# A scan mixer computed in blocks of four time steps, inside a fused two-block decoder kernel

## Chip, cores and metric

One core of a Trainium2 chip. The time is device microseconds of one execution of the whole program (both decoder blocks, two layers each, 256 tokens, float32 results). Engines are named as in the profile: PE is the matrix engine, PEld its weight loads, DVE the vector engine, ACT the scalar engine, POOL GpSimd, SP the engine that issues most transfers.

## The reference, cut to what matters

The first block (`first_block`, two layers of attention with a selector, a state-space mixer and a gated MLP) isn't touched by the change. The second block has three mixers side by side on one normalised input: latent attention, gated linear attention (GLA) and S5, a diagonal state-space scan:

```python
def s5_mixer(u, lam_re, lam_im, b_re, b_im, c_re, c_im, d, log_dt, w_glu, b_glu):
    lam = lax.complex(jnp.minimum(lam_re, -1e-4), lam_im)          # 32 groups x 64 states
    lam_bar = jnp.exp(lam * jnp.exp(log_dt)[:, None])
    b_bar = ((lam_bar - 1.0) / lam)[..., None] * lax.complex(b_re, b_im)
    bu = ...                       # (L, 32 groups, 64 states), complex, from 16 channels a group
    _, states = lax.associative_scan(diag_combine, (lam_bar, bu), axis=1)  # x[t] = lam_bar x[t-1] + bu[t]
    y = Re(states) @ c_re - Im(states) @ c_im + d * u
    y = jax.nn.gelu(y)
    return y * jax.nn.sigmoid(y @ w_glu + b_glu)
```

There are 256 steps, 512 channels (32 groups of 16) and 2048 complex states (16 tiles of 128 partitions, each two groups).

## The kernel before, in words

**Stages.** `Plan` cuts all weight matrices into 658 units in eight stages, `STAGES`: a b a b (first block, layers 0 and 1), then c d c d (second block). Stage c holds the mixers, d the MLP. Stage c has 79 units. Ten of them, the `native` ones, multiply plain float32; each of the others is 24 matmuls (high times high, high times low, low times high part of a float32 product split in two). A unit's weights come by DMA into `ring` (5 slots); ACT copies them to `WH` (function `hi`, rounding them to the high part), DVE subtracts to get `WL` (function `lo`, line 1403), PE multiplies. `WH` and `WL` have four halves, so `hi` of unit u+3 waits for PE to have finished unit u-1. Where `x.pool` holds, POOL makes `WL` in DVE's place (line 2115); that is so for 11 units of each stage b.

**Order.** Each engine's program is one loop over the units. At unit u it does its part of the unit, the evacuation of groups that ended one to three units ago, and then the steps of the mixers that `agenda` lists for u. `C_TICKS` and `A_TICKS` name the units at which each mixer advances, counted from the stage's first unit. Each mixer is a generator on each engine (`s5`, `gla`, `norms`, `heads`), and a `yield` ends its step for this tick. So all engines walk the same list, and each runs its queue strictly in order. A step that waits holds up everything behind it on its engine, `hi` and `lo` of the next units too.

**S5 before.** The setup `s5set` (in the stage ahead: stage b for layer 0, stage d for layer 1; ticks 48 to 62 and 38 to 52) makes the step's decay `r`, its turn (cos, sin), the output matrix `SC5` times the input factor, and two tables of 16 powers of the turn (lines 1925 to 1942) in `TF`. POOL's `turns` multiplies these into the 256 turns of each state tile, `CT`: 12 instructions of 128x256 for each q (lines 2101 to 2105). In stage c, `s5` takes the 16 state tiles in 8 pairs q, four ticks each (ticks 6 to 55 of 79). For each tile PE multiplies the input (`inputs`: two matmuls 32x128 by 256 columns), DVE turns the result back (lines 1956 to 1959), scans it over 256 steps twice (line 1962), turns it forward (lines 1970 to 1973), and PE multiplies with `SC5` (`y`, 32 columns of output for each tile). DVE then adds the skip term (line 1981), and gelu and the gate follow (lines 1985 to 1991, ACT's `tanh`). The result is first read by `glu` at unit 65.

**Lines named later.** 1519 and 1520 sum squares for the next stage's norm; 1536 spreads `pe`, the shared rope part of the keys (unit 9), to eight heads; 1540 evacuates `b1`, GLA's output projection, and frees its bank; 1781 is a step of GLA; 1606 scales the attention weights; 955 loads an activation table.

Of the kernel before, what the change touches and what calls it, by code (L numbers as in the profile page):

```python
# [30 lines left out]
def vec_columns():  # L31
    at, n = {}, 0
    for l in range(2):
        for name, k in VECS:
# [7 lines left out]
          ("mask", 384), ("cos2", 256), ("sin2", 256), ("scan", 256), ("invf", 1), ("eps", 1)]  # L42
# [10 lines left out]
def const_array():  # L53
# [7 lines left out]
    put["id"][:] = p == f[:, :128]  # L61
    put["ones"][:] = 1
# [117 lines left out]
def stage_c(l):  # L180
# [20 lines left out]
    return (su + cq + ckv + pe + glr + gq + gk + gv + gr + uq + uk + uv + g[1] + b[1] + g[0] + g[2] + b[0] + glu  # L201
# [11 lines left out]
class Plan:  # L213


    def __init__(self):
# [31 lines left out]
        for x in self.units:  # L248
            b = self.base[x.stage + 1] - self.base[x.stage]
            x.pool = x.split and STAGES[x.stage][0] is stage_b and x.i - self.base[x.stage] < 44 and x.i % 4 == 3  # L250
# [55 lines left out]
def turn_ticks(first, n, num, den):  # L306
# [19 lines left out]
    "s5": turn_ticks(6, 32, 8, 5) + [57, 58, 59, 60, 61],  # L326
}
S5_TICKS = {stage_b: [48, 50, 52, 54, 56, 58, 60, 62], stage_d: [38, 40, 42, 44, 46, 48, 50, 52]}


def program(nc, io):
# [3 lines left out]
    with ctx:  # L335
# [78 lines left out]
        for nm, n in (("QH", 2048), ("KH", 2048), ("VV", 1024), ("OA", 1024), ("CQ", 768), ("CKV", 512), ("GQ", 512),  # L414
# [6 lines left out]
        a2["OG"], a2["MG"] = a2["GK"], a2["GV"]  # L421
# [5 lines left out]
        SU, TF, CT = ar(a2["SU"], 4, T), ar(a2["TF"], 4, 256), ar(a2["CT"], 2, 2, 512)  # L427
        SC5, SB5, SX = ar(a2["SC5"], 2, 512), ar(a2["SB5"], 2, 512), ar(a2["SX"], 512)
        SG = trig[:, 0, :].rearrange("p (a b) -> p a b", b=16)
        MG, GX, G2 = ar(a2["MG"], 8, T), ar(a2["GX"], 8, T), ar(a2["QH"], 8, T)  # L430
        BRH = [over("oah", a2["VV"], 4), over("ogh", a2["KT"], 4), over("ysh", a2["TF"], 4)]
        BRL = [over("oal", a2["OA"], 4), over("ogl", a2["OG"], 4), over("ysl", a2["CT"], 4)]
# [96 lines left out]
        def tensor_program(e):  # L529
# [154 lines left out]
            def gla(l):  # L684
                L, st = LA, 4 + 2 * l
                p.wait_ge(ev_scalar("glr", l, 0, st), wgate_in(l))
# [67 lines left out]
            def heads(l, par):  # L754
                L = (LB, LA)[par]
                m = 4 + l
                for bi in (par, par + 2):
# [8 lines left out]
            def s5(l):  # L766
                L = LC

                def inputs(q, h):
                    R = slice(32 * ((2 * q + h) % 4), 32 * ((2 * q + h) % 4) + 32)  # L770
                    p.wait_ge(ev_scalar("su", l, q // 4, 4 + 2 * l), s5_in(l))
                    for i in range(2):
# [14 lines left out]
                for q in range(8):  # L787
                    if q:
                        p.wait_ge(L.V("scan", l, q - 1, 0), L.V("scan", l, q - 1, 1))
                        y(q - 1)  # L790
# [1450 lines left out]
```

## Time and profile before

| what | value |
|---|---|
| median of 3 runs | 2397.68 us (2396.55 to 2397.8) |
| the profiled execution | 2392.69 us |
| its span, first to last instruction | 2390.6 us |
| PE busy | 2229.1 us, 93% |
| DVE busy | 1783.4 us, 75% |
| ACT busy | 1350.0 us, 56% |
| POOL busy | 277.0 us, 12% |
| mean granted PE clock | 0.971 of full |

The profiled execution is the one that all rows come from. Its time stands 2.1 us above its span (start and end of the program) and 5.0 us under the median. A busy PE is one with a matmul in flight; matmuls overlap, so the time that one costs is the distance to the start of the next, and not its own duration. The stages end, by the first activation of each boundary, near 1324 us (stage c of layer 0 starts), 1666 us (its stage d), 1858 us (stage c of layer 1) and 2202 us (its stage d).

### The profile page before, as it was taken

How to read it: one execution, taken by the hardware profiler on the slowest of the kernel's cores; microseconds unless marked ns; L12 is line 12 of the kernel's file. 1: busy time of each engine (PE TensorE's matmuls, PEld its weight loads, DVE VectorE, ACT ScalarE, POOL GpSimd, SP SyncE). 2: the span in 40 equal slices, each digit the busy share in tenths (PEclk: the TensorE clock that was granted, in tenths of full speed). 3: DMA queues.
4: the chain of work that ended last, by engine and by line, in shares of the span. 5: the costliest groups of instructions: out<-in, count | busy, mean ns of one | idle time of the engine just before them, and what ended most of it. 6: DMA issues, size and time to landing. Idle time of an engine off the chain costs nothing.

```text
span 2390.6 us, 42135 instructions
## 1 busy us (share of the span) xinstructions
PE 2229.1 (93%) x17214; PEld 2083.8 (87%) x17214; DVE 1783.4 (75%) x3196; ACT 1350.0 (56%) x2113; POOL 277.0 (12%) x308
## 2 busy tenths in 40 slices
PE   2989999999999999999999899898999999898999
PEld 2979899989998898998998875788999875788999
DVE  5898778678769877776778788876668788876653
ACT  3577886466446888854664535454554435444542
POOL 0000000022000000000211332300004232200000
PEclk9999999999999999999999998999999998999999
DMA  7555456567755554664665313244655313244554
GB/s 278 174 165 181 160 202 220 181 198 232 231 178 168 160 201 145 210 221 143 190 193 172 126 60 108 89 158 136 197 184 187 119 54 117 89 159 133 185 186 132
DMA packets 110850, 395.72 MB, mean 166 GB/s; under 512 B 12321, under 2 KB 13889, under 8 KB 110401
## 3 DMA queue, kind: packets, MB, share of 16 engines
q1 hardware_dynamic: 96768, 343.52, 44.1%
q0 software_dynamic: 12160, 44.08, 5.7%
q10 hardware_dynamic: 1728, 5.43, 0.6%
q8 instruction: 136, 2.23, 0.4%
q14 instruction: 58, 0.47, 0.1%
HBM read 391.93 MB, written 1.05 MB: 164 GB/s over the span
## 4 chain that ended last, share of the span: by engine, by line
PE 74%; DVE 14%; ACT 8%; issue 2%; DMA 1%; SPq 0%; DVEq 0%; ACTq 0%
PE bank L534 73%; ACT scr L966 3%; DVE WL L1403 3%; ACT WH L966 2%; ACT L955 2%; DMA ring<-in_w 1%; DVE arena L1467 1%; DVE scr L1656 1%; DVE arena L2022 1%; ACT arena L966 0%; DVE scr L1450 0%; DVE small L1655 0%; DVE scr L1643 0%; DVE arena L1581 0%; DVE scr L1970 0%
## 5 line engine op out<-in xcount | busy, mean ns | idle before, releaser
L966 ACT ACTIVATE WH<-ring 128x1024 fp32r<-128x1024 f32 (+1 forms) x638 | 671.1, 1053 | 865.9 <-PE bank L534 837.8
L534 PE MATMUL bank<-HTH,WH 128*128 128x256 f32 x3392 | 984.9, 290 | 39.2 <-DVE HTL L1443 12.3
L534 PE MATMUL bank<-HTL,WH 128*128 128x256 f32 x3392 | 971.2, 286 | 0.0
L534 PE MATMUL bank<-HTH,WL 128*128 128x256 f32 x3392 | 970.5, 286 | 0.0
L1403 DVE TENSOR_TENSOR WL<-ring,WH 128x1024 fp32r<-128x1024 f32 (+2 forms) x616 | 747.7, 1224 | 150.8 <-ACT WH L966 149.1
L534 PEld LDWEIGHTS bank<-HTH,WH 128*128 128x128 f32 x3392 | 662.7, 195 | 60.5 <-issue 48.9
L534 PEld LDWEIGHTS bank<-HTL,WH 128*128 128x128 f32 x3392 | 662.7, 195 | 1.7 <-issue 1.4
L534 PEld LDWEIGHTS bank<-HTH,WL 128*128 128x128 f32 x3392 | 662.3, 195 | 0.0
L955 ACT ACT_TABLE_LOAD x110 | 141.1, 1283 | 21.8 <-DMA arena<-in_crow 13.8
L534 PE MATMUL bank<-ff2h,WH 128*128 128x256 f32 x512 | 144.0, 281 | 0.0
L534 PE MATMUL bank<-ff2l,WH 128*128 128x256 f32 x512 | 143.8, 281 | 0.0
L534 PE MATMUL bank<-ff2h,WL 128*128 128x256 f32 x512 | 143.8, 281 | 0.0
L2123 POOL DMA_DIRECT2D arena<-in_wada x80 | 42.9, 536 | 840.9 <-DVE mod L2022 779.7
L534 PE MATMUL bank<-scr,cst 128*128 128x256 f32 (+2 forms) x190 | 71.8, 500 | 64.5 <-ACT scr L966 54.3
L2022 DVE CUSTOM_DVE_ANT_0 arena<-arena 128x1024 f32<-128x1024 f32 x96 | 116.4, 1221 | 9.3 <-DMA arena<-in_wada 9.3
L2101 POOL TENSOR_TENSOR arena<-arena 128x256 f32<-128x256 f32 x64 | 63.4, 990 | 505.4 <-DVE scr L1973 289.6
L1467 DVE SCALAR_TENSOR_TENSOR scr<-bank,cols,scr 128x254 f32<-128x254 f32 (+1 forms) x176 | 72.7, 476 | 49.8 <-ACT scr L966 49.8
L534 PE MATMUL bank<-arena 64*128 64x128 f32 (+8 forms) x608 | 98.5, 342 | 8.9 <-DVE arena L1981 6.7
L534 PEld LDWEIGHTS bank<-scr,cst 128*128 128x128 f32 (+1 forms) x190 | 33.6, 198 | 83.3 <-ACT scr L966 59.2
L534 PE MATMUL bank<-ff1h,WH 128*128 128x256 f32 x352 | 100.3, 285 | 0.5 <-DVE WL L1403 0.5
L534 PE MATMUL bank<-ff1l,WH 128*128 128x256 f32 x352 | 99.5, 283 | 0.0
L534 PE MATMUL bank<-ff1h,WL 128*128 128x256 f32 x352 | 99.4, 282 | 0.0
(284 smaller groups left out, 3852.1 us busy)
## 6 DMA issues: line engine op xcount, KB each, us to landing
ring<-in_w SPq DMA_DIRECT2D x620, 512.0 KB, 4.0
arena<-in_wada POOLq DMA_DIRECT2D x80, 512.0 KB, 4.6
ring<-in_w SPq DMA_DIRECT2D x16, 384.0 KB, 3.9
arena<-in_wada SPq DMA_DIRECT2D x8, 512.0 KB, 19.7
arena<-in_wada ACTq DMA_DIRECT2D x8, 512.0 KB, 22.3
ring<-in_w SPq DMA_DIRECT2D x8, 288.0 KB, 2.8
arena<-in_s POOLq DMA_DIRECT2D x4, 512.0 KB, 5.2
cst<-in_cst SPq DMA_DIRECT2D x1, 1025.0 KB, 6.5
```

Source lines behind the costliest of these rows:

```text
L534: ins = e.matmul(out, a, b, start=(start and i == 0), stop=(stop and i == len(pairs) - 1))
L955: e.add_instruction(mybir.InstLoadActFuncSet(name=f"I-{4000000 + table[1]}", act_func_set_id=need, ins=[], outs=[]))
L966: return e.activation(out, a, func, **kw)
L1403: e.tensor_tensor(half(WL, x), raw(x), half(WH, x).bitcast(F32), ALU.subtract).then_inc(lo_vector.inc(x.i), 1)
L1467: ins = e.scalar_tensor_tensor(outs[h][:, d:T], ps[:, h * T:h * T + T - d], col(name + "_w", l, (ntap - 1 - d) * nch + cs[h]), outs[h][:, ...
L1656: serial(e.match_replace(y, top, x, GONE), L.V)
L2022: e.tensor_tensor_reduce(tile, tile, silc, 1.0, 0.0, ALU.mult, ALU.add, mod[:, l, j:j + 1]).then_inc(ada_vec.inc("sum", l, j), 1)
L2101: e.tensor_tensor(o, slow(a), fast(b), ALU.mult).then_inc(S.inc(), 1)
L2123: e.dma_start(adabuf, io["wada"][before[0], before[1]]).then_inc(ada_in.inc(*before, by=16), 16)
```

## The change

S5 is computed in 64 blocks of four steps.

- The scans run over 64 block states with the decay r^4, on tiles of 8 state tiles side by side (512 columns), twice instead of sixteen times. The table of turns `TAB` has 64 entries a state, is made by DVE's `s5set` by doubling (n = 1 to 32), and POOL's `turns` is gone.
- The inputs of four steps are stacked: `U` holds 4 steps x 2 groups x 16 channels on 128 partitions and 64 columns. POOL's `powers` makes B, lam B, lam^2 B, lam^3 B (`BS`, 18 instructions of 128x256 in the stage ahead), ACT spreads them to `PADB`, PE transposes (32 transposes), ACT copies to `BT`. `CS` holds C lam^1 to C lam^4 (24 instructions of 128x256 on DVE), spread by ACT to `PADC`.
- What an output takes from inputs of its own block comes from a triangular matrix of short answers: PE makes C lam^k B (`kernel`, 32 matmuls of 32 columns), DVE masks it and adds d (`kernel_`), ACT shifts it into `TM`.
- `y` is three matmuls a tile (48 of 63 or 64 columns), ACT takes the result to `SU` (`out`, 16 copies of 32 partitions).
- Ticks: `s5` 2 to 36 instead of 6 to 61, `s5set` 4 to 56 (stage b) or 4 to 44 (stage d) in 14 steps instead of 8. `tanh` is two ACT steps of 128x512, at ticks 30 and 32, instead of four of 128x256.
- POOL clears three arena tiles of 2048 at the start of stage c, and one at unit 11; ACT's first step (tick 2) waits for the first three.
- `pe` moves from unit 9 to unit 26, between the query and the key projections.
- POOL makes `WL` for 7 units of each stage c (15, 18, 21, 33, 36, 39, 42).

```diff
-    return (su + cq + ckv + pe + glr + gq + gk + gv + gr + uq + uk + uv + g[1] + ...
+    return (su + cq + ckv + glr + gq + gk + gv + gr + uq + pe + uk + uv + g[1] + ...
+            x.pool = x.split and (STAGES[x.stage][0] is stage_b and u < 44 and x.i % 4 == 3
+                                  or STAGES[x.stage][0] is stage_c and 15 <= u < 45 and u % 3 == 0)
-    "s5": turn_ticks(6, 32, 8, 5) + [57, 58, 59, 60, 61],
+    "s5": [2, 3, 4, 5, 6, 7, 8, 9, 10, 12, 13, 14, 16, 17, 18, 19, 20, 21, 22, 24, 25, 26, 28, 30, 32, 34, 36],
-S5_TICKS = {stage_b: [48, 50, 52, 54, 56, 58, 60, 62], stage_d: [38, 40, 42, 44, 46, 48, 50, 52]}
+S5_TICKS = {stage_b: [4, 6, 8, 11, 14, 17, 20, 23, 26, 29, 33, 37, 50, 56],
+            stage_d: [4, 6, 8, 10, 12, 14, 16, 18, 20, 22, 25, 28, 38, 44]}
...
+                def inputs(h):                                   # PE, ticks 8 and 12
+                    for n in range(8):
+                        t = 8 * h + n
+                        for i in range(2):
+                            ins = mm(L.b[i][:, 64 * n:64 * n + 64], [(BT[i][:, t, :], U[:, t, :])])
+                def y(h, b):                                     # PE, ticks 18 and 24
+                        mm(b[:, 64 * n:64 * n + 64], [(TM[:, t, :], U[:, t, :])], start=(n == 0), stop=False)
+                        ins = mm(b[:, 64 * n + 1:64 * n + 64], [(PADC[0][:, t, :], xr[:, n, 0:63]),
+                                                               (PADC[1][:, t, :], xi[:, n, 0:63])], ...)
...
+                p.wait_ge(L.G("zero", l), L.G("bs", l))          # ACT, tick 2
+                spread(PADB[0], BS[:, 0], "pad", l, 0)
...
+                def scans(h):                                    # DVE, ticks 12, 13 and 19, 20
+                    for out, src in ((a2_, a0), (a0, a1)):
+                        for n in range(8):
+                            ins = e.tensor_tensor_scan(v2(out, 8)[:, n, :], r4[:, t:t + 1].to_broadcast([128, 64]),
+                                                       v2(src, 8)[:, n, :], 0.0, ALU.mult, ALU.add)
...
+                    if at == 0:                                  # POOL, first unit of stage c
+                        e.memset(ar(a2["QH"], 2048), 0.0).then_inc(S.inc(), 1)
+                        e.memset(ar(a2["KH"], 2048), 0.0).then_inc(S.inc(), 1)
+                        e.memset(ar(a2["VV"], 2048), 0.0).then_inc(S.inc("zero", l), 1)
-                        turns(l, range(2, 8))
```

## Rows read from the trace of the kernel before

**Rows 1.** The page's first part: busy us (share of the span), instructions.
```profile
PE 2229.1 (93%) x17214; PEld 2083.8 (87%) x17214; DVE 1783.4 (75%) x3196; ACT 1350.0 (56%) x2113; POOL 277.0 (12%) x308
```

**Rows 2.** Windows by stage (b, c, d, c): length, then busy us of each engine, granted clock.
```profile
core 0: us, PE busy (x) PEld busy (x) DVE busy (x) ACT busy (x) POOL busy (x), PEclk, DMA share, GB/s
1120.00:1324.00 204.00, 193.74 (x1580) 192.09 (x1579) 147.98 (x337) 115.13 (x177) 47.54 (x36) 0.98 0.57 176
1324.00:1666.00 342.00, 309.52 (x2128) 267.22 (x2128) 271.43 (x446) 162.47 (x261) 66.83 (x77) 0.94 0.36 113
1666.00:1858.00 192.00, 187.69 (x1542) 186.81 (x1542) 130.76 (x252) 93.57 (x120) 27.16 (x27) 0.98 0.57 182
1858.00:2202.00 344.00, 312.48 (x2128) 270.10 (x2128) 270.26 (x446) 163.01 (x263) 64.63 (x74) 0.93 0.35 113
```

**Rows 3.** The same columns for four stretches of 20 us in layer 0's stage c.
```profile
1385.00:1405.00 20.00, 16.33 (x111) 13.75 (x110) 19.61 (x32) 5.22 (x7) 7.25 (x10) 0.78 0.37 119
...
1445.00:1465.00 20.00, 17.05 (x50) 8.09 (x48) 11.74 (x19) 11.70 (x19) 7.11 (x9) 0.73 0.30 93
...
1505.00:1525.00 20.00, 17.49 (x114) 16.18 (x114) 16.00 (x45) 11.38 (x25) 2.41 (x3) 0.83 0.25 80
1525.00:1545.00 20.00, 16.44 (x115) 14.13 (x116) 19.06 (x31) 5.27 (x10) 10.04 (x12) 0.91 0.26 80
```

**Rows 4.** Waits in 1324 to 1666: who <- whom, total us, times, longest.
```profile
PE bank L534 <- ACT scr L966: 6.6, 3, 2.9
PE bank L534 <- DVE arena L1981: 3.4, 2, 3.0
PE bank L534 <- DVE arena L1540: 3.1, 1, 3.1
PE bank L697 <- DVE scr L1781: 2.9, 1, 2.9
PE bank L605 <- DVE scr L1606: 2.0, 2, 1.3
PE bank L534 <- DVE scr L1973: 1.9, 2, 1.1
PE bank L534 <- DVE arena L1536: 1.6, 1, 1.6
```

**Rows 5.** PE in order of time: start us, duration, form, records.
```profile
1345.78 1.13 PE L534 MATMUL bank<-arena 32*128 32x256 f32 x4
1346.83 0.38 PE L534 MATMUL bank<-HTH,WH 128*128 128x256 f32 x1
...
1370.61 1.06 PE L534 MATMUL bank<-scr,arena 128*32 128x256 f32 x8
1371.61 1.13 PE L534 MATMUL bank<-arena 32*128 32x256 f32 x4
...
1423.53 1.22 PE L534 MATMUL bank<-arena 128*128 128x128 f32 x10
1424.59 0.43 PE L534 MATMUL bank<-scr,cst 128*128 128x256 f32 x1
```

**Rows 6.** DVE groups in 1324 to 1666: form, count, busy, mean ns, idle before.
```profile
L1403 DVE TENSOR_TENSOR WL<-ring,WH 128x1024 fp32r<-128x1024 f32 x69 | 85.3, 1243 | 14.0 <-ACT WH L966 13.8
L1962 DVE TENSOR_TENSOR_SCAN scr<-small,scr 128x256 f32<-128x256 f32 x16 | 10.2, 679 | 0.3
L1956 DVE TENSOR_TENSOR scr<-bank,arena 128x512 f32<-128x512 f32 x16 | 11.0, 689 | 5.6 <-PE bank L534 5.4
```

**Rows 7.** POOL groups of the whole span, same columns.
```profile
L2115 POOL TENSOR_TENSOR WL<-ring,WH 128x1024 fp32r<-128x1024 f32 x22 | 54.7, 2488 | 300.1 <-ACT WH L966 300.1
...
L2134 POOL MEMSET arena<- 128x1024 f32 x2 | 1.9, 971 | 16.0 <-DVE HTL L1443 16.0
```

**Rows 8.** The end of layer 0's setup in order of time; brackets: idle before, releaser.
```profile
1304.14 0.17 DVE L1942 TENSOR_SCALAR small<-small 128x16 f32<-128x16 f32 x1
...
1307.14 1.22 PE L534 MATMUL bank<-scr,cst 128*128 128x256 f32 x2 [5.09 <-DVE scr L1520]
```

**Rows 9.** ACT around a table load, in order of time.
```profile
1471.53 1.28 ACT L955 ACT_TABLE_LOAD   x1
1472.82 0.42 ACT L966 ACTIVATE scr<-scr 128x256 f32<-128x256 f32 x1
```

**Rows 10.** A window at layer 0's stage boundary, columns as in rows 2.
```profile
1300.00:1323.00 23.00, 15.57 (x108) 14.49 (x106) 15.02 (x36) 7.65 (x10) 18.07 (x21) 0.85 0.54 181
```

More of the change, by code:

```diff
@@ L61, in const_array @@
     put["id"][:] = p == f[:, :128]
+    put["same"][:] = p % 32 // 16 == f[:, :32] // 16
     put["ones"][:] = 1
@@ L802, in s5 @@
+                for i in range(4):
+                    yield
+                p.wait_ge(L.V("turned", l, 1))
+                y(1, L.b[0])
+                yield
+                for i in range(7):
                     yield
@@ L1317, in s5set @@
                 yield
-                for i in range(5):
+                for i in range(11):
                     yield
@@ new lines, in tanh @@
+                def tanh(cp):
+                    p.wait_ge(L.V("gelu", l, cp))
+                    act(L.s[cp], L.s[cp], ACT.Tanh, scale=float(np.sqrt(2 / np.pi))).then_inc(L.A.inc("tanh", l, cp), 1)
+                p.wait_ge(L.G("zero", l), L.G("bs", l))
+                spread(PADB[0], BS[:, 0], "pad", l, 0)
+                yield
+                spread(PADB[1], BS[:, 1], "pad", l, 1)
+                yield
+                p.wait_ge(L.A.now())
+                channels(0, 0)
+                yield
@@ L1337, in s5 @@
+                channels(0, 1)
+                yield
+                channels(1, 0)
+                yield
+                channels(1, 1)
                 yield
                 yield
-                p.wait_ge(L.V("ys", l, 3), L.G("ct", l, 7))
+                pairs = [(i, j) for i in range(4) for j in range(i, 4)]
+                p.wait_ge(L.V("km", l))
+                shifts(pairs[0:4])
+                yield
+                shifts(pairs[4:7])
+                yield
+                shifts(pairs[7:10])
@@ L1340, in s5 @@
+                out(1, 2, L.b[0])
+                yield
+                out(1, 3, L.b[0])
+                yield
+                yield
+                tanh(0)
+                yield
+                tanh(1)
+                yield
+                yield
+                p.wait_ge(L.V("ys", l, 1))
                 for j in range(2):
@@ L2008, in s5 @@
                 yield
                 yield
-                gelu(3)
+                for r in range(4):
+                    steps(r)
+                    yield
+                kernel_()
+                yield
+                yield from back_turn(0)
+                yield from scans(0)
+                yield from turn(0)
+                yield from back_turn(1)
+                yield from scans(1)
+                yield from turn(1)
+                yield
+                yield
+                gelu(0)
@@ L2164, in program @@
     return [x.block for x in units]
+S5_ORDER = [4 * c + r for r in range(4) for c in range(4)]
 def pack_vec(name, a, k):
```

452 lines of the change are left out of this document (262 added, 190 removed), and 2 rows, old and new, of the table IK.

## Prediction

> **What bounds the kernel now.** I began with the page's busy times: PE is busy 93% of the span, DVE 75%, ACT 56% [rows 1]. So PE sets the time, and work taken from DVE is worth only what PE waits for it. Next come the windows by stage [rows 2]. The MLP stages (b and d) have PE busy 193.7 of 204 and 187.7 of 192 us at a granted clock of 0.98. The mixer stages (c) have it busy 309.5 of 342 and 312.5 of 344 us, at 0.94 and 0.93. All that this change can win lies in the 686 us of the two stages c, and they are alike, so I work out one and double it.
>
> Inside a stage c the stretches of 20 us [rows 3] show two different troubles. In 1385 to 1405, and in 1525 to 1545, DVE is busy 19.6 and 19.1 of 20 us, and PE only 16.3 and 16.4: there DVE is late. In 1445 to 1465 neither DVE nor ACT is full, but PE has short native units and its clock is 0.73. The table of waits names whom PE waits for [rows 4]: lines 1981 (S5's output), 1540 (a bank to be freed), 1781 (GLA), 1973 (S5's states), 1536 (the copy of `pe`) and 1606 (attention weights), all on DVE, 14.9 us in sum, and 6.6 us for ACT. DVE is busy 271 of 342 us [rows 2], with 85.3 in line 1403 [rows 6]. S5's own lines in this window (1956 to 1991) take some 105 us: the largest are 16 reads of a bank at 689 ns and 32 scans at 679 to 771 ns [rows 6].
>
> **The clock.** After each of these stalls the granted clock is at its lower level (1.2 instead of 2.4 GHz) for a while. A window with a mean clock of 0.78 has lost 20 x 0.22 = 4.4 us of PE's rate, those of 0.83 and 0.91 lose 3.4 and 1.8 [rows 3]. These three hold the waits for lines 1781, 1981 and 1540. So a stall of 3 us costs nearer to 6, where PE is the bound behind it.
>
> **The change, part by part**, for one stage c.
>
> *PE's own work.* Removed: 16 times `inputs`, each 1346.83 - 1345.78 = 1.05 us from its start to the next unit's; and 8 times `y`, each 1371.61 - 1370.61 = 1.00 us [rows 5]. Together 24.8 us at the full clock. Added: 32 transposes, 32 matmuls of 32 columns, 32 of 64 and 48 of 64. Plain float32 matmuls leave two records each, so these are 64 + 64 + 96 = 224 records. The nearest row with full 128x128 weights and few columns (64 and 128 mixed) has 10 records from 1423.53 to 1424.59, 0.106 us each [rows 5]; I take 0.10, as most of the new ones have 64 columns or fewer. The least would be a cost in proportion to the columns: 4 records of 256 columns in 1.05 us, 0.26 each, so 0.066 for 64. The most is 0.125, that of 8 records of 256 columns by 32 output columns in 1.00 us. A transpose I take at 0.12, by the same row. Sum: 224 x 0.10 + 32 x 0.12 = 26.2, so **+1.4 us** (bounds -6 to +7). PE's matmul work thus doesn't shrink, though four times fewer columns stream: a matmul of 64 columns with its own 128x128 weights costs nearly what it cost with 256.
>
> *Fewer stops.* S5 interrupts the run of units 24 times now and 7 times then. The first matmul behind a stop lasts 0.38 instead of some 0.28 us and the next starts 0.1 us later; at about 0.1 us for 17 stops, **-1.5 us**.
>
> *DVE.* Removed: some 105 us. Added: 16 copies into `U` and the small ones (some 7 us, at up to 0.4 each), 2 x 12 instructions of 512 columns at 0.69 (16.5 us), 32 scans of 64 (bounds 0.17, a quarter of 679, and 0.25: 7 us), gelu and gates 5 us, the mask 2 us: about 37 us. Seven `WL` at 1.24 us go to POOL, 8.7 us more [rows 6]. DVE falls from 271 to about 195 us. But in ticks 12 to 22 the new steps stand densely (about 2 us a tick), beside GLA's chain; the relief there is a third, and it is nearly whole after unit 24. So I take, of the waits [rows 4]: all of 1981 (-3.4) and 1973 (-1.9), as S5's output no longer passes there on DVE; 2.4 of the 2.9 for 1781; 2.1 of the 3.1 for 1540, since four S5 instructions of 0.69, 0.69, 0.42 and 0.42 us stand ahead of it, and the rest of its lateness comes from an attention step that waits for ACT; 1.0 of 2.0 for 1606; and 1536 goes from where it is (-1.6). Sum **-12.4 us**.
>
> *Clock.* Of the 9.6 us in the three windows I take two thirds, **-6.5 us**; between 1445 and 1465 the cause is the native units, and it stays.
>
> *POOL.* `turns` goes (66.8 us of busy POOL in the stage [rows 2]); three clears of 2048 cost twice 0.97 each [rows 7], 5.8 us after the last `HTL`, and ACT's first step waits for them at tick 2. Behind that wait in ACT's queue stands `hi` of unit 6. PE then still has the three opening units and unit 3 to run, over 11 us at the lower clock of the start, so I charge 0.5. POOL's `WL` takes 2.49 us instead of 1.24 [rows 7] and is begun three units ahead: nothing.
>
> *ACT.* Added some 28 us in units 2 to 25 (four spreads, eight copies of channels, ten shifts, sixteen outputs), where it is half idle. The two `tanh` at ticks 30 and 32 fall between steps of `heads` that need another table: up to four loads at 1.28 us [rows 9] and 1.2 us of work, just where native units are short and PE already waits for ACT (6.6 us [rows 4]). I charge **+2**. `pe`'s copy (2.3 us on DVE) now frees its bank among short units: **+1.5**, about what it costs today.
>
> The Trainium skill speaks against this part: its page "ScalarE: Activation LUTs", section "What ACT_TABLE_LOAD costs", puts a switch at 1.28 us of load plus about 1.38 us of drain. The row shows the load's 1.28 and the next activation 0.01 us behind its end, so the trace has no such drain. By the page's figure the four loads would cost 5.5 us more, if all of it lay on PE's path.
>
> Sum for one stage c: 1.4 - 1.5 - 12.4 - 6.5 + 0.5 + 2 + 1.5 = -15.0; twice, **-30 us**.
>
> *The setup*, once a layer. In layer 0 its last table step ends at 1304.14, and behind it lie the square sums that PE waits for: 5.09 us [rows 8], followed by the lower clock (0.85 over 23 us, 3.4 us [rows 10]). The new setup ends 12 units before the end of the stage, and POOL's turns, which at that time slow DVE's two-input instructions, are gone: -8.5. In layer 1 PE doesn't wait there. The new setup's DVE work is about 28 us instead of 23 and stands mostly among the `up` units, where DVE is busy 70%; PE has 1 to 3 us of slack a step: **+1.5** in all.
>
> Total: -30 - 8.5 + 1.5 = -37. Against the profiled execution's 2392.7 that is 2355.7. The median of the runs stands 5.0 above that execution, so I forecast 2397.7 - 37 = 2360.7, rounded **2360 us**.
>
> **Rivals.**
>
> *DVE was behind everything in the mixer* (chance 0.24). For it: DVE is at 19 to 19.6 of 20 in each stretch before a PE stall. Then all 14.9 us of DVE waits, part of the ACT waits, and all 9.6 us of clock go, and PE's new matmuls cost 5 us less than I said: about -26 a stage, -60 in all: **2337**.
>
> *ACT takes DVE's place* (0.18). S5 moves some 28 us to ACT, in a part where ACT also serves GLA; a GLA or attention step on DVE waits for ACT and holds `lo` back as DVE's own work did. The waits change their name, half of my -12.4 and -6.5 is lost, and the table loads cost 4: -3.5 a stage with the rest, -14 in all: **2384**.
>
> *No effect but the boundary's, given back* (0.05). The stalls are latencies of chains and not backlog: -1 a stage, and the setup costs in stages b and d what the boundary wins: **2395**.
>
> *Slower* (0.07). PE starves at the start of stage c. ACT's spreads wait for POOL's clears and block `hi`; PE's transposes wait for the spreads, ACT's copies for the transposes, `kernel` for those, and DVE's `kernel_` at tick 8 for `kernel`, with `lo` behind it. The chain has six hand-overs between ticks 2 and 12 where there was one. At 3 us each and half as much again for the clock it costs 27 us a stage, against 15 won: 2 x 12 - 7 = +17: **2415**. It decides from where PE's waits in the first twelve units exceed 18 us a stage. Against it: every hand-over is spaced two ticks (6 us) apart.
>
> *The table switch by the page's figure* (0.02): the Trainium skill's rule of "ScalarE: Activation LUTs" above. As a mechanism of this kernel: ACT would stand still after each of the extra loads as long as the load itself lasts, 4 x 1.28 = 5.1 us a stage in the short units, 10 in all: **2370**. No row shows it.
>
> **How the numbers follow.** My own case (2348 to 2375) has 0.44, the others 0.24, 0.18, 0.05, 0.07 and 0.02. The unknown price of a small matmul alone moves the sum by -15 to +11, the clock term by +-7, the waits by +-8. The range is **2332 to 2391**: it takes in my case, ACT's and most of DVE's. 0.2% (4.8 us) is about what a measurement of this kernel can tell from no change. Faster by more: 0.44 + 0.24 + 0.18 + 0.02 = 0.88; within: 0.05; slower: 0.07.
>
> **What would show it right or wrong.** In the profile after: stage c about 324 us instead of 342, DVE busy in it 190 to 200; no PE wait for an S5 line after unit 24, 1781 and 1540 under 1 us; the clock of stage c at 0.96 or above; the PE wait of 5.09 us at the first boundary gone; the small matmuls at 0.07 to 0.12 us a record. It is wrong if small matmuls cost 0.15 or more, if ACT is the new releaser of PE's waits, if DVE in stage b is over 90% busy and PE waits for `WL` there, or if the transposes wait for `pad`.

## The result, and the profile after

The changed kernel takes **2420.7 us** (median of 4 runs, 2417.2 to 2422.2) against 2397.1 us for the kernel before (4 runs on the same chip, 2395.5 to 2397.8): ratio 1.0103, 95% interval 1.0089 to 1.0117. It is 1% slower. I had forecast 2360 us with a range of 2332 to 2391, and gave 7% to "slower" by a mechanism that turned out not to be it. One slip in the text ahead of the prediction: the two `tanh` steps stand at ticks 28 and 30, not 30 and 32.

The profiled execution took 2420.92 us with a span of 2419.1. The first part of its page, then the windows by stage (b, c, d, c, the columns of rows 2):

```profile
PE 2255.9 (93%) x17470; PEld 2142.2 (89%) x17470; DVE 1680.3 (69%) x2998; ACT 1417.4 (59%) x2203; POOL 194.8 (8%) x176
```

```profile
1124.00:1339.00 215.00, 197.18 (x1590) 194.70 (x1590) 172.02 (x350) 119.44 (x183) 50.60 (x33) 0.98 0.52 165
1339.00:1683.00 344.00, 316.48 (x2256) 290.47 (x2256) 200.24 (x340) 195.33 (x305) 28.14 (x13) 0.92 0.35 113
1683.00:1882.00 199.00, 190.66 (x1542) 189.56 (x1542) 143.15 (x256) 93.18 (x118) 17.06 (x22) 0.97 0.55 173
1882.00:2228.00 346.00, 316.98 (x2256) 291.56 (x2256) 203.84 (x342) 195.49 (x305) 28.08 (x13) 0.92 0.35 112
```

Against [rows 2], DVE in stage c fell from 271 to 200 us in layer 0 and 204 in layer 1, about what I had said (190 to 200). But PE's busy time there rose from 309.5 to 316.5 us and the granted clock fell from 0.94 to 0.92. And in stage b DVE rose from 148 to 172 us.

For the comparison of kernels I cut each trace at the first activation that writes `HTH` in a stage. That gives lengths, in us:

| kernel | b, layer 1 | c, layer 0 | d, layer 0 | c, layer 1 | d, layer 1 |
|---|---|---|---|---|---|
| before | 206.1 | 342.3 | 191.8 | 343.6 | 189.5 |
| changed | 214.3 | 344.4 | 199.2 | 345.5 | 191.0 |
| setup late | 204.4 | 345.3 | 192.6 | 344.4 | 192.2 |
| no powers | 209.1 | 342.8 | 189.8 | 342.2 | 192.2 |
| tanh late | 214.7 | 343.0 | 200.0 | 342.7 | 192.2 |
| matmuls spread | 214.7 | 336.3 | 199.9 | 336.3 | 189.5 |
| answers only spread | 214.3 | 340.2 | 200.0 | 341.6 | 191.0 |
| wide answers | 214.8 | 336.3 | 199.9 | 336.1 | 192.0 |
| three edits | 202.9 | 331.7 | 193.7 | 328.9 | 189.5 |
| three, powers late | 208.3 | 332.4 | 192.5 | 334.0 | 192.1 |
| three, early tanh, no POOL `WL` in c | 204.4 | 338.6 | 192.6 | 336.4 | 191.0 |
| three, no POOL `WL` in c | 204.4 | 330.1 | 191.1 | 330.9 | 192.1 |
| the same, powers on DVE | 205.8 | 328.5 | 189.9 | 328.4 | 192.2 |
| the same, no POOL `WL` at all | 208.7 | 329.1 | 191.1 | 331.0 | 192.0 |

The stages of the first block, whose code is the same in all of them but one (the last gives POOL's `WL` of stage b back to DVE), took 435.0 to 439.6 us (each a) and 196.9 to 200.4 (its first b): the lower clock falls now here, now there. So a single stage is known to some 2 to 4 us, and these untouched stages make 7 of the 28 us between the two profiled spans. What the change itself cost is +8.2 in stage b, where the boundary's stall went as well, +7.4 in stage d, and +2 in each stage c where I had forecast -15. The first two are surer than one profile makes them: the five kernels with the same setup (changed, tanh late, matmuls spread, answers only spread, wide answers) give 214.3 to 214.8 and 199.2 to 200.0.

**Stage b: DVE is full.** Four windows of 20 us in the changed kernel, in the part of the stage where the new setup runs:

```profile
1165.00:1185.00 20.00, 16.16 (x120) 16.02 (x121) 19.40 (x34) 9.86 (x17) 10.65 (x8) 0.91 0.44 145
1185.00:1205.00 20.00, 19.13 (x160) 18.95 (x159) 19.76 (x32) 10.73 (x17) 14.51 (x14) 1.00 0.54 168
1205.00:1225.00 20.00, 15.40 (x127) 15.06 (x126) 19.13 (x43) 10.84 (x19) 4.69 (x2) 1.00 0.42 132
1225.00:1245.00 20.00, 18.28 (x151) 17.93 (x150) 19.34 (x56) 11.42 (x20) 5.53 (x2) 1.00 0.60 181
```

DVE (third engine column) is busy over 19 of 20 us in all four, and PE stands idle for 11 of the 80. PE's largest waits in this stage, from the table of waits (total, times, longest):

```profile
PE bank L543 <- DVE scr L1576: 13.2, 9, 3.6
PE bank L543 <- DVE HTL L1549: 2.9, 1, 2.9
```

Line 1576 reads the banks of the MLP's `up` groups: PE waits for a bank that DVE has not emptied. In the kernel before, this reader is line 1467:

```profile
PE bank L534 <- DVE scr L1467: 1.3, 1, 1.3
```

The stage had 5.1 us of wait for the square sums [rows 8] besides. The square sums' wait is gone, the reader's is ten times as long. In stage d of layer 0 the setup makes DVE late for something else, the low halves of the weights, for which PE didn't wait there before:

```profile
PE bank L543 <- DVE WL L1512: 4.9, 2, 3.9
```

**What makes it full.** DVE in order of time at the start of the setup's large steps, and POOL at the same moment:

```profile
1166.82 0.42 DVE L2024 TENSOR_TENSOR scr<-arena,small 128x256 f32<-128x256 f32 x1
...
1167.82 0.42 DVE L2027 TENSOR_TENSOR scr<-arena,small 128x256 f32<-128x256 f32 x1
1168.28 2.52 DVE L2028 TENSOR_TENSOR arena<-scr 128x256 f32<-128x256 f32 x1
1170.72 0.84 DVE L2029 SCALAR_TENSOR_TENSOR arena<-scr 128x256 f32<-128x256 f32 x1
1171.59 1.52 DVE L1512 TENSOR_TENSOR WL<-ring,WH 128x1024 fp32r<-128x1024 f32 x1
```

```profile
1166.57 3.94 POOL L2269 TENSOR_TENSOR WL<-ring,WH 128x1024 fp32r<-128x1024 f32 x1 [7.10 <-ACT WH L1010]
1170.46 1.57 POOL L2258 TENSOR_TENSOR trig<-arena,small 128x256 f32<-128x256 f32 x2
1171.99 2.17 POOL L2258 TENSOR_TENSOR arena<-arena,small 128x256 f32<-128x256 f32 x2
```

Line 2028 is a subtraction of two 128x256 tiles. It takes 0.42 us where POOL leaves DVE alone (experiment 1), and 2.52 us here, until 0.3 us after POOL's subtraction has ended. But lines 2024 to 2027, four products with two inputs as well, ran at their 0.42 inside the same POOL subtraction, and it was that subtraction that got longer: 3.94 us, where its mean before was 2.49 [rows 7]. So I read these rows as turns and not as an even slowing: POOL stood while DVE's products followed each other, and then DVE stood until POOL was done. Beside POOL's powers the turns are short: in the steps of 1187 and 1200 us DVE's instructions take 0.84 to 0.96 us each instead of 0.42, and POOL's of lines 2258 to 2261 some 0.8. Over the whole stage the setup's lines (1985 to 2073) keep DVE busy for 38.6 us, and for 29.1 in experiment 1; the mean of POOL's eleven subtractions is 3.05 us. The Trainium skill's page "GPSIMD Engine Reference", section "Key points", says that GpSimd shares its SBUF interfaces with VectorE and contends with instructions that have two SBUF inputs. The trace agrees: in these rows every instruction that got longer, on DVE and on POOL, has two inputs in SBUF.

**Stage c: the clock falls with PE busy.** PE from 1370 us, in order of time (96 records of the short answers and of `inputs(0)` drawn together in one line), and three windows of 15 us around it:

```profile
1370.21 0.28 PE L543 MATMUL bank<-HTH,WL 128*128 128x256 f32 x1
1370.33 15.20 PE L543 MATMUL bank<-arena 128*128 128x32 f32 x96
1385.29 0.56 PE L543 MATMUL bank<-HTH,WH 128*128 128x256 f32 x1
```

```profile
1355.00:1370.00 15.00, 14.73 (x126) 14.73 (x127) 10.79 (x20) 12.53 (x19) 0.00 (x0) 1.00 0.54 168
1370.00:1385.00 15.00, 15.00 (x100) 15.00 (x98) 5.47 (x10) 1.91 (x4) 0.00 (x0) 0.71 0.28 88
1385.00:1400.00 15.00, 15.00 (x101) 14.74 (x101) 6.92 (x11) 9.32 (x15) 0.00 (x0) 0.84 0.13 48
```

PE doesn't wait for anything here: its busy time is 15.00 of 15. In the window before it was 14.73, and all that is missing is the end of a wait at 1355.27, 21 us ahead of the fall. Yet the clock goes from 2.4 to 1.2 GHz at 1376.2 and stays there for 13.7 us, of which 9 are the run of small matmuls and the rest the unit behind it. The Trainium skill's page "TensorE: Matmul & The Clock Gate", section "HAM oscillation — how this bites in real kernels", puts such falls down to stretches in which PE stands idle. No idle stretch stands in the 20 us ahead of this one. The measurement decides, and the runs below show that it goes with the run of small matmuls itself.

The waits of PE in this stage, to be held against [rows 4]:

```profile
PE bank L543 <- ACT scr L1010: 8.3, 2, 4.5
PE bank L614 <- DVE scr L1715: 3.4, 2, 2.1
PE bank L543 <- DVE HTL L1659: 3.3, 1, 3.3
PE bank L543 <- DVE HTL L1552: 2.7, 1, 2.7
PE bank L543 <- DVE arena L1645: 2.7, 1, 2.7
PE bank L543 <- DVE oal L1668: 2.4, 2, 2.1
PE bank L706 <- DVE scr L1890: 1.9, 1, 1.9
PE bank L783 <- ACT arena L1010: 1.1, 1, 1.1
PE bank L543 <- DVE arena L1649: 0.9, 1, 0.9
```

S5's own lines are gone. The line numbers answer so: 1649 was 1540 (3.1 us then), 1890 was 1781 (2.9), 1645 was 1536 (`pe`, 1.6), 1715 was 1606 (2.0).

### The profile page after: what moved, and what is told of

It is laid out like the page before. It is cut to its first block, busy times and chain, and to the rows that moved or that the text cites. A ratio compares the mean times of both kernels' runs of the same rounds, so it can differ in the third digit from the quotient of the medians.

```text
span 2419.1 us, 42409 instructions
## 1 busy us (share of the span) xinstructions
PE 2255.9 (93%) x17470; PEld 2142.2 (89%) x17470; DVE 1680.3 (69%) x2998; ACT 1417.4 (59%) x2203; POOL 194.8 (8%) x176
## 4 chain that ended last, share of the span: by engine, by line
PE 74%; DVE 13%; ACT 9%; issue 3%; DMA 1%; SPq 0%; DVEq 0%; ACTq 0%
PE bank L543 73%; ACT scr L1010 3%; DVE WL L1512 2%; ACT WH L1010 2%; ACT L999 2%; DMA ring<-in_w 1%; DVE arena L1576 1%; ACT arena L1010 1%; DVE scr L1576 1%; DVE scr L1765 1%; DVE arena L2185 1%; DVE scr L1559 1%; PE bank L614 0%; DVE small L1764 0%; DVE scr L1752 0%
## 5 line engine op out<-in xcount | busy, mean ns | idle before, releaser
L1512 DVE TENSOR_TENSOR WL<-ring,WH 128x1024 fp32r<-128x1024 f32 (+2 forms) x602 | 739.0, 1237 | 211.7 <-ACT WH L1010 209.4
L543 PEld LDWEIGHTS bank<-HTH,WH 128*128 128x128 f32 x3392 | 669.5, 197 | 68.8 <-issue 51.1
L999 ACT ACT_TABLE_LOAD x120 | 154.0, 1283 | 28.6 <-DMA arena<-in_crow 13.5
L2269 POOL TENSOR_TENSOR WL<-ring,WH 128x1024 fp32r<-128x1024 f32 x36 | 99.0, 2749 | 528.1 <-ACT WH L1010 528.1
L1010 ACT ACTIVATE arena<-bank 128x512 f32<-128x512 f32 (+4 forms) x168 | 90.6, 549 | 58.7 <-PE bank L543 57.9
L543 PE MATMUL bank<-arena 128*128 128x64 f32 (+8 forms) x800 | 110.8, 317 | 2.1 <-DVE arena L1925 1.2
L543 PEld LDWEIGHTS bank<-arena 128*128 128x128 f32 (+3 forms) x800 | 92.4, 203 | 10.8 <-issue 2.7
L1010 ACT ACTIVATE scr<-scr 128x256 f32<-128x256 f32 (+3 forms) x181 | 86.0, 500 | 24.4 <-DVE scr L1576 21.7
```

The source lines that it names most:

```text
L543: ins = e.matmul(out, a, b, start=(start and i == 0), stop=(stop and i == len(pairs) - 1))
L999: e.add_instruction(mybir.InstLoadActFuncSet(name=f"I-{4000000 + table[1]}", act_func_set_id=need, ins=[], outs=[]))
L1010: return e.activation(out, a, func, **kw)
L1512: e.tensor_tensor(half(WL, x), raw(x), half(WH, x).bitcast(F32), ALU.subtract).then_inc(lo_vector.inc(x.i), 1)
L2269: e.tensor_tensor(half(WL, x), raw(x), half(WH, x).bitcast(F32), ALU.subtract).then_inc(lo_gpsimd.inc(x.i), 1)
```

## The experiments

Each kernel was timed side by side with the kernel before, whose median was then 2393.6 to 2396.9 us; ratios are to it. Experiments 1 to 6 make one edit each to the changed kernel.

**1. The setup moved late.**

```diff
-S5_TICKS = {stage_b: [4, 6, 8, 11, 14, 17, 20, 23, 26, 29, 33, 37, 50, 56],
-            stage_d: [4, 6, 8, 10, 12, 14, 16, 18, 20, 22, 25, 28, 38, 44]}
+S5_TICKS = {stage_b: [4, 6, 8, 42, 44, 46, 48, 50, 52, 54, 56, 58, 60, 61],
+            stage_d: [4, 6, 8, 34, 36, 38, 40, 42, 44, 46, 48, 50, 52, 54]}
```

The diff is cut: the products of the setup's steps also go to free tiles of `arena` instead of `scr`, and its last part waits for POOL's powers.

> The changed kernel, with the setup of the scan mixer moved: its first three steps stay, its eleven steps of 128x256 work and tables go from units 11 to 56 of stage b to units 42 to 61 (stage d: from 10-44 to 34-54); its products lie in free arena tiles. Theory 'load' (in stages b and d VectorE has no room before unit 42, where it also makes most of the low halves of the weights, and TensorE waits for it): stage b of layer 1 gets shorter by 6 to 12 us and stage d of layer 0 by 3 to 7, the whole comes to 2400-2412 us, and VectorE's 20 us windows in the middle of stage b fall from over 19 to under 18.5. Rival 'amount' (what costs is that there are more VectorE instructions at all, wherever they stand): the time stays within 3 us of 2420.7 and the waits move with the steps. Rival 'clock' (the stage is longer because of where the lower clock falls): the stage's gaps fall but not its length.

Measured: **2404.2 us** (2400.3 to 2404.9), ratio 1.0033 (1.0020 to 1.0046). Stage b got 9.9 us shorter, stage d 6.6. The same stretch of 80 us in one window, first of the changed kernel, then of this one:

```profile
1165.00:1245.00 80.00, 68.97 (x551) 67.95 (x552) 77.63 (x162) 42.85 (x71) 35.37 (x24) 0.98 0.50 157
```

```profile
1165.00:1245.00 80.00, 80.00 (x669) 80.00 (x668) 60.71 (x106) 50.89 (x84) 32.78 (x26) 1.00 0.60 189
```

PE no longer waits in this stretch. "Load" holds, and not "amount": the same instructions cost next to nothing in the later units. "Clock" fell, as the stage's length went with its waits. A full DVE by itself isn't what costs, though: in 1261 to 1281 and 1281 to 1301, where the steps now stand, DVE is busy 19.47 and 19.11 of 20 us, and PE 20.00 in both. In these units DVE has no bank of line 1576 to empty (no such instruction in the 40 us, 45 of them in the 80 us of the changed kernel above). The instructions also became cheaper. One of the four products that make a power of C and the first of the two sums behind them, by line and form (count, busy, mean ns), in the changed kernel and here:

```profile
L2034 DVE TENSOR_TENSOR scr<-arena,small 128x256 f32<-128x256 f32 x4 | 2.5, 630 | 0.0
L2038 DVE TENSOR_TENSOR arena<-scr 128x256 f32<-128x256 f32 x4 | 4.7, 1162 | 0.1
```

```profile
L2033 DVE TENSOR_TENSOR arena<-arena,small 128x256 f32<-128x256 f32 x4 | 1.7, 416 | 0.0
L2037 DVE TENSOR_TENSOR arena<-arena 128x256 f32<-128x256 f32 x4 | 1.7, 426 | 0.1
```

The edit takes the steps out of the busy units and out of POOL's way at once, so by itself it doesn't part load from contention.

**2. No powers on POOL.** The six instructions of each of the three steps are replaced by two clears; B's powers are left out.

```diff
-                for m, x, y in ((m0, re, a), (m1, im, b), (m2, re, b), (m3, im, a)):
-                    e.tensor_tensor(m, x, y, ALU.mult).then_inc(S.inc(), 1)
...
+                e.memset(BS[:, 0, :, 16 * i:16 * i + 16], 0.0).then_inc(S.inc(), 1)
```

> The changed kernel with GpSimd's three steps of powers of B (six 128x256 two-input instructions each) replaced by clears of the same tiles: B's powers are left out. Theory 'contention' (GpSimd's two-input instructions slow VectorE's beside them, and that makes VectorE late): stages b and d lose half or more of the 8.2 and 7.4 us that they are longer than in the kernel before, the time is 2408-2413 us. Theory 'load': VectorE's own work is what is too much, the 0.75-1.02 us instructions of GpSimd are a small part of it, the time is 2416-2421 us.

Measured: **2406.9 us** (2402.5 to 2408.5), ratio 1.0053 (1.0036 to 1.0070); 14 us under the changed kernel. Stage b lost 5.2 us, stage d 9.4. The two sums of a step, the first of them the line above whose mean was 1162 ns:

```profile
L2038 DVE TENSOR_TENSOR arena<-scr 128x256 f32<-128x256 f32 x4 | 1.7, 424 | 0.1
L2039 DVE TENSOR_TENSOR arena<-scr 128x256 f32<-128x256 f32 x4 | 3.9, 973 | 0.0
```

The second rose, from a mean of 550: one of its four, at 1206.27, stands 2.64 us beside a `WL` subtraction of POOL, and line 2028 still takes 2.52. These long ones come of POOL's `WL` and not of the powers; what the powers had doubled, the products, is back at 0.42. So "contention" holds, the time 1 us under its range: DVE has not one instruction less here, and its setup lines take 33.4 us instead of 38.6. But DVE was still busy 75.4 of the 80 us in 1165 to 1245, and PE 73.7. Load and contention are two parts of one cause: DVE has little room early in a stage b, and beside POOL's work its own gets longer. (The profiled execution was the fastest of the four, and its stages c are shorter too, by 1.6 and 3.4 us, for which nothing here gives a reason.)

**3. Tanh late.** The last six ticks of `s5` at 34, 37, 41, 45, 49, 53.

> The changed kernel with the last six ticks of the scan mixer at units 34, 37, 41, 45, 49 and 53 instead of 26 to 36, so that the two tanh (with two table loads each) stand at 37 and 41, among the other steps of stage c. Theory 'tables' (the two PE gaps of 4.85 and 4.12 us in stage c, with ScalarE named as releaser, come of the tanh and the table loads falling beside the softmax and norm steps of these units): both gaps fall under 2 us, and each stage c gets shorter by 3 to 6 us, the time is 2409-2416 us. Rival 'total' (ScalarE has this work somewhere in any case, and the gaps move to units 37 to 41): the time stays within 3 us of 2420.7.

Measured: **2416.7 us** (2411.4 to 2420.4), ratio 1.0090 (1.0071 to 1.0109). Not settled by itself: 4 us better, but the runs overlap with those of the changed kernel, and the two gaps of layer 0 only fell from 4.47 and 3.84 us to 3.11 and 3.56, and not under 2 (the 4.85 and 4.12 of the text on record aren't PE's waits in the profile). Experiment 8 takes it up again.

**4. Small matmuls spread.** The 32 matmuls of the short answers in four parts of 8, at four successive ticks; the 24 of the first half's output in four parts of 6; ACT's two `out` steps of that half three ticks later.

```diff
+                def answers(part):
+                    for t in range(4 * part, 4 * part + 4):
+                        ins = mm(LB.b[1][:, 32 * t:32 * t + 32], ...)
...
-                y(0, LB.b[1])
-                yield
                 for i in range(4):
+                    y(0, LB.b[1], range(2 * i, 2 * i + 2))
                     yield
```

> The changed kernel with its two densest runs of small matmuls cut up: the 32 matmuls of the matrix of short answers go in four parts of 8 to four successive ticks, the 24 of the first half's output in four parts of 6. Theory 'dense' (the lower clock of 13.7 us that begins within the run of 96 records at 1376 us, with no wait ahead of it, comes of the run itself): these two stretches of lower clock get shorter or go, each stage c gains 2 to 6 us, the time is 2409-2417 us. Rival 'phase' (lower clock falls as often wherever small matmuls stand; their amount decides): the lower clock moves but its sum in stage c stays within 7 us, the time is 2418-2423 us.

Measured: **2405.0 us** (2401.7 to 2406.6), ratio 1.0041 (1.0026 to 1.0056). Both stages c got shorter, by 8.1 and 9.2 us, more than I had expected. The window of the first:

```profile
1338.00:1674.00 336.00, 307.58 (x2256) 282.60 (x2256) 198.12 (x341) 195.10 (x306) 28.15 (x13) 0.95 0.36 115
```

The same 2256 records, hardly a change in DVE and ACT, but PE is busy 307.6 us instead of 316.5, at 0.95 instead of 0.92. The answers and `inputs(0)` now take 3 x 1.71 + 6.74 = 11.9 us, counted from start to start, instead of 15.0:

```profile
1357.88 1.87 PE L543 MATMUL bank<-arena 128*128 128x32 f32 x16
...
1364.29 1.87 PE L543 MATMUL bank<-arena 128*128 128x32 f32 x16
...
1368.95 1.87 PE L543 MATMUL bank<-arena 128*128 128x32 f32 x16
...
1373.62 6.98 PE L543 MATMUL bank<-arena 128*128 128x32 f32 x48
```

The rest of the 8 us goes with the lower clock, which in a stage c went from 54 us to 34 and 31; PE's waits grew a little (27.8 to 28.6 and 28.4 to 30.4 us). So "phase" fell. How much of it falls at one place differs even so: at the answers it was 6.8 us in layer 0, and none in layer 1, where the same code stands.

**5. Only the answers spread.**

> The changed kernel with only the 32 matmuls of the short answers cut into four parts of 8; the first half's output stays in one run. Theory 'dense' : the lower clock that began at 1376 us within the run of 96 records gets shorter or goes, the one of 13.7 us at the output (1427 us) stays; each stage c gains 2 to 5 us of the 8 to 9 that both cuts gave, 2409-2415 us. Rival 'one of them' (only the cut of the output counted, as the run that stands behind a wait): 2418-2422 us.

Measured: **2414.4 us** (2409.3 to 2416.1), ratio 1.0085 (1.0069 to 1.0101). Stages c lost 4.2 and 3.9 us, half of what both cuts gave. The lower clock of the answers shrank from 13.7 to 6.8 us, that of the output stayed at 13.7. Each dense run has its own.

**6. Wide answers.** One pair of matmuls of 512 columns in place of 16 pairs of 32; the short answers are left out.

```diff
-                for t in range(16):
-                    ins = mm(LB.b[1][:, 32 * t:32 * t + 32], ...)
+                ins = mm(LB.b[1][:, :], [(PADB[i][:, 0, :], C0[:, i, :, :].unsqueeze(2).to_broadcast([128, 16, 2, 16]))
+                                         for i in range(2)])
```

> The changed kernel (2420.7 us) with one pair of matmuls of 512 columns in place of the 16 pairs of 32 columns of the short answers (the answers are left out: the bank holds other values). Theory 'dense small matmuls lower the clock': 60 records of 0.112 us go, 6.7 us less what the wide ones take, some 5 us a stage, and the lower clock of 13.7 us at 1376 us shrinks to 7 or less, another 3 us: stage c shorter by 7 to 9 us each, 2403-2408 us. Rival 'the price alone' (the lower clock there has another cause): 4 to 5 us a stage, 2410-2413 us.

Measured: **2402.3 us** (2393.6 to 2407.0), ratio 1.0023 (1.0005 to 1.0040). Stages c lost 8.1 and 9.4 us. Sixty records fewer, at 0.112 us, are 6.7 us, and the lower clock of that place shrank to 6.8 us, later, at 1394. The run of the output still drew 17.1 us of it, behind a wait of 4.3 us that was 1.9. So the answers as written, 64 records with 32 columns, cost some 8 to 9 us a stage, about what three full-width units cost.

**7. Three edits together** (1, 3 and 4).

> The changed kernel with three edits together: the setup moved behind unit 42 of stage b and unit 34 of stage d, the answers and the first half's output cut into four parts each, and the last six ticks at units 34 to 53. Theory 'three causes' (VectorE's load in stages b and d, the dense runs of small matmuls in stage c, and the tanh beside other ScalarE work are separate causes, each in its own stages): the gains of the single runs add up, 2420.7 less 16.5, 15.7 and 4.0 is 2384, less if part of each was where the lower clock fell; 2379 to 2389 us, and so below the kernel before. Rival 'given back' (each gain came from a shift of the lower clock that another edit shifts again): 2393-2404 us.

Measured: **2381.1 us** (2373.5 to 2382.6), ratio 0.9951 (0.9935 to 0.9968). The gains add up, and the kernel is 0.5% faster than the one before. "Given back" fell.

**8. Early tanh.** The kernel of experiment 10 (three edits, and no `WL` on POOL in stage c) with the last six ticks back at 26 to 36.

> The kernel of 2374.8 us with the scan mixer's last six ticks back at units 26 to 36. Theory 'tables' (two tanh with their table loads cost PE's time where they stand beside heads steps): 3 to 6 us slower, 2378-2381 us. Rival 'hidden': within 2 us of 2374.8, and the 4 us that the late tanh gave alone was within what the lower clock's place makes.

Measured: **2384.5 us** (2378.9 to 2387.9), ratio 0.9959 (0.9944 to 0.9973), against 2374.8 with the late ticks: 9.7 us, more than I had expected, from an edit that showed only 4 by itself. The first stage c of both, early, then late:

```profile
1326.00:1665.00 339.00, 309.89 (x2258) 284.72 (x2258) 200.88 (x350) 195.57 (x306) 9.35 (x6) 0.94 0.36 114
```

```profile
1330.00:1660.00 330.00, 304.01 (x2258) 279.32 (x2258) 200.37 (x348) 189.56 (x302) 9.35 (x6) 0.96 0.36 117
```

ACT has 6.0 us less with the same arithmetic; 5.1 of it are table loads, 12 instead of 16 in the stage, at 1.28 us each [rows 9]. With the late ticks the wait for `pe`'s copy falls from 2.7 to 0.9 us, that for attention's weights from 3.4 to 2.0, and the two gaps behind ACT from 4.36 and 3.84 to 2.88 and 3.56; all waits of layer 0's stage c fall by 2.9 us and those of layer 1's by 4.4. Not all of the difference is the `tanh`'s, though. The early kernel has 6.8 us of lower clock from 1364.7 on, at the answers, ahead of any `tanh`, and the late one has none there: up to 3.4 of the 8.5 us in layer 0 may be where the lower clock fell. So "tables" is shown, and its price, 3 to 6 us forecast and 9.7 measured, isn't known better than some 6 to 10. Where the loads stood in the changed kernel is seen in ACT's order of time:

```profile
1491.18 1.28 ACT L999 ACT_TABLE_LOAD   x1
...
1495.97 1.28 ACT L999 ACT_TABLE_LOAD   x1
1497.27 0.63 ACT L1010 ACTIVATE scr<-scr 128x512 f32<-128x512 f32 x1
1499.76 1.28 ACT L999 ACT_TABLE_LOAD   x1 [0.43 <-PE bank L543]
```

The `tanh` at 1497.27 stands between two steps of `heads`, with a load on either side.

**9. Three edits, and POOL's powers late** (units 44, 46, 48 and 32, 35, 38).

> As the kernel with the three edits, and GpSimd's steps of powers at units 44, 46 and 48 of stage b (behind the last low half that GpSimd makes there) and at 32, 35 and 38 of stage d, instead of 14, 18 and 22. Theory 'contention' (leaving the powers out gave stage d 9.4 us, more than moving VectorE's steps gave it): stages b and d lose a further 2 to 5 us together, 2376-2382 us. Rival 'moved contention' (the powers now stand beside VectorE's setup steps and slow these): the same as with the three edits or up to 5 us more.

Measured: **2385.8 us** (2378.3 to 2389.1), ratio 0.9963 (0.9951 to 0.9976). "Contention" missed here: no gain, and stage b came out 5.4 us longer than with the three edits alone. "Moved contention" had the number, and for stage b its mechanism too. The setup's first step of 128x256 work (lines 2032 to 2037) now stands beside the powers, and all six instructions take 839 to 964 ns instead of 416 to 426:

```profile
L2032 DVE TENSOR_TENSOR arena<-arena,small 128x256 f32<-128x256 f32 x1 | 0.8, 843 | 0.0
```

The step takes 4.9 us (1256.00 to 1260.90) instead of 2.2, the `WL` behind it comes late, and PE waits 1.9 us for it at 1262.5, where it didn't wait before. The steps of C's powers (lines 2042 to 2047), which come after POOL is done, stayed at 417 to 425 ns. The rest of the 5.4 goes with the lower clock: 10.2 us of it in this stage instead of 3.4, half of what is new right behind this wait.

**10. Three edits, and no `WL` on POOL in stage c.** (The text on record says ten of each stage; there are seven.)

> As the kernel with the three edits, but GpSimd makes no low halves of weights in stage c; VectorE makes these ten of each stage again. Theory 'VectorE has room in stage c' (its busy share there is about two thirds): within 3 us of the kernel with the three edits. Rival 'VectorE late' : stages c get longer by 2 us or more each, 5 to 10 us in all. Rival 'slowed' (GpSimd's 2.75 us subtractions slow VectorE more than they relieve it): 3 to 8 us faster.

Measured: **2374.8 us** (2374.3 to 2375.4), ratio 0.9923 (0.9908 to 0.9938). The medians are 6 us apart, the profiled spans (2372.5 and 2371.7) and the sums of the two stages c (661.0 and 660.6) are not; but the profiled execution with the three edits was the fastest of its four, at 2373.5 us. So POOL's help in stage c is worth nothing; whether it costs the 6 us, as "slowed" says, stays open.

**11. The same, with the powers on DVE** in three setup steps of their own.

> The three edits without GpSimd's low halves in stage c (2374.8 us), and the powers of B made by VectorE in three setup steps of its own (units 36, 38, 40 of stage b, 28, 30, 32 of stage d) instead of by GpSimd at units 14, 18 and 22. Theory 'contention' (what GpSimd's two-input instructions take from VectorE is more than the same work costs on VectorE): 18 instructions of some 0.42 us, 7.6 us more of VectorE a setup, and still 1 to 6 us faster, 2369-2374 us. Rival 'amount': 2376-2382 us.

Measured: **2370.9 us** (2368.1 to 2372.9), ratio 0.9907 (0.9892 to 0.9921). 18 more instructions on DVE a setup, and the time is not longer. The intervals overlap with experiment 10's, and stages b and d moved by +1.4 and -1.2 us, so a gain from it isn't shown; "amount" is refuted. This is the fastest version: 23 us under the kernel before, timed beside it (2394.4), and some 50 under the changed one.

**12. The same as 10, with no `WL` on POOL at all.**

> The same kernel of 2374.8 us, with GpSimd making no low halves in stages b either (eleven of each stage b go back to VectorE). Theory 'contention' (a 2.5 us subtraction of GpSimd slows VectorE by as much as the 1.24 us that it takes off it): within 3 us of 2374.8. Rival 'amount': in stages b VectorE is busy 18 to 19 of 20 us and needs the relief; 2380-2395 us. Rival 'slowed': stages b get shorter by 1 to 3 us each, 2368-2372 us.

Measured: **2380.8 us** (2378.4 to 2383.4), ratio 0.9949 (0.9934 to 0.9964). POOL's help in stages b is worth 4.3 us in layer 1 (208.7 against 204.4), where the setup stands, and nothing in layer 0. "Amount" was right, at the low end of its range.

## Why the prediction was wrong

In stage c the change's idea was worth about what I had said. With its setup, its `tanh` and its small matmuls put elsewhere, and no `WL` on POOL, a stage c takes 328 to 331 us instead of 342 and 344: -12 to -15 where I had forecast -15. The whole didn't follow: the fastest version won 23 us and not 37, as its stage b stayed at 205.8 against 206.1. What I mis-sized is what the places cost in which the change puts these things. Between the two profiles my sum is 65 us off: 34 of it in the two stages c, 16 in stage b, 7 in stage d, and 9 in stages that the change doesn't touch.

- **The setup, +1.5 forecast, and -8.5 for the boundary.** The stall at the boundary went, as forecast. But the term for the work itself, +1.5 for both layers, was far too small, and it is the step that failed first: stage b +8.2 with the stall of 5.1 us and, perhaps, the 3.4 of clock behind it gone, so +13 to +17 gross, and stage d +7.4. I reasoned from DVE's 70% average in the `up` units and from its sum of instructions (28 us instead of 23), at their undisturbed 0.42 us. Undisturbed that sum is right (29.1 us in experiment 1); in the changed kernel the same lines take 38.6, with means of 0.55 to 1.16 us for those of C's powers, and the windows show DVE at 96% to 99%. I had even used POOL's slowing of DVE as a gain at the boundary; I didn't apply it to the units where POOL makes `WL` and now the powers too. The sign I had named for being wrong, DVE in stage b over 90% busy with PE waiting for `WL` there, came in part: DVE is over 90% in four windows, but 80% over the stage; PE waits there for the banks of line 1576, and for `WL` only in stage d.
- **Clock in stage c, -6.5 forecast.** I took the clock to follow from PE's waits. Where that holds I was right: outside the two dense runs the lower clock fell from 44.4 to 27.0 us in layer 0, worth 8.7. But each dense run drew 13.7 us of it, the first with no wait ahead, the second behind one of 1.9 us (line 1890). In sum it rose from 44.4 to 54.4, some +5, and in layer 1 from 50.9 to 54.6, some +2. This is the largest error in stage c: 11.5 us in layer 0 and 8.4 in layer 1.
- **PE's own work, +1.4 - 1.5 forecast.** Nearly right in size at full clock: 32 records of `inputs(1)` take 3.59 us and 48 of `y(1)` 5.3, 0.11 each where I had taken 0.10. What is left of layer 0's +2.1 when the waits and the clock are taken off is 0 to +2.
- **Waits, -12.4 on DVE, +2 and +1.5 for ACT and `pe`.** Measured by line, in layer 0, as changes in us: S5's 1981 and 1973 -5.3 (as said), 1540 -2.2 (-2.1 said), 1781 -1.0 (-2.4 said), 1606 +1.4 (-1.0 said), `pe` +1.1 (-0.1 said, net), ACT and `pad` +2.8 (+2.5 said with POOL's clears). Sum of these -3.2 instead of -8.4. The relief that I gave to lines that aren't S5's own mostly didn't come, and the waits for the attention weights and for `pe` grew; both shrink again when the `tanh` and its loads are moved away (experiment 8).
- **POOL's clears and the chain of hand-overs** ("Slower", 2415): the time was near by luck, the mechanism wrong. The transposes wait 1.1 us for `pad`, not 3 us at each of six hand-overs.
- **"DVE was behind everything"** (2337) is refuted: DVE lost 71 us in the stage and these waits only 3.
- **The table switch** (2370): the four extra loads came, 16 in the stage instead of 12, but ACT doesn't stand still behind them: 1491.18 and 1.28 us of load, and the next activation starts at 1492.48, 0.02 us later.
- **"ACT takes DVE's place"** (2384) named a part of it: ACT's share of the waits rose. It isn't what made the kernel slower.

The general failing: the sum went by the amount of work on each engine, and the losses came by place. I read stages c in stretches of 20 us, but stages b and d, into which the change moves work, only as a whole.

## What to carry to other kernels

Before you move side work into another stage, read that stage in windows of a few units, not its average, ask which of its readers PE waits for there, and price each two-input vector instruction at what it takes beside GpSimd's, where both run. Treat a run of many matmuls with few columns (here 96 and 48 records) as work that can take the PE clock down even if PE never waits: cut it up among the full-width ones. And put an activation that needs another table where its neighbours share it; its loads are paid by whoever waits behind it.

## What the runs showed of the hardware

- Two-input f32 instructions of DVE and POOL hold each other up. DVE's 128x256 instruction takes 0.42 us undisturbed, 0.84 to 0.96 beside POOL's 128x256 ones, and 2.52 at worst beside POOL's 128x1024 subtraction. That subtraction takes 2.49 us on average before, 3.05 in this stage b, and 3.94 where four DVE products ran through it at 0.42 each.
- A DVE that is busy 19.1 to 19.5 of 20 us didn't stop PE (20.00 of 20, experiment 1), and one at 19.1 to 19.8 did (11 of 80 us), where PE's banks waited for it.
- A plain f32 matmul with its own 128x128 weights costs 0.11 us a record for 32 and for 64 columns at the full clock, two records each (16 records in 1.71 us, 32 in 3.59).
- The granted clock fell to 1.2 GHz inside a run of 96 such records with PE busy 15.00 of 15 us. Cutting two such runs in four took 20 and 24 us of lower clock and 8 and 9 us of time from the two stages. Why they bring the clock down isn't shown.
- POOL's clear of 128x2048 takes 1.81 us, twice the 0.97 of 128x1024 [rows 7] within a tenth.
